# Down and out products with tokens as the stationary operand and rows turned back, a re-ordered first attention, and spread context scaling, in a two-block transformer kernel on one NeuronCore

## The chip, the core and the metric

The kernel runs on one core of one Trainium2 chip. The metric is the device time of one execution in microseconds (us), lower is better. TensorE multiplies matrices; the profile calls its matmuls PE and its loads of the stationary operand PEld. VectorE is DVE, ScalarE is ACT, GpSimd is POOL, and SyncE (SP) issues most of the DMA loads.

## What is computed

256 tokens of width 1024, all in float32, pass through two blocks. The first has two layers. What matters here of them:

```python
def swiglu_ffn(x, w_in, w_out):
    gate, up = jnp.split(x @ w_in, 2, axis=-1)
    return (jax.nn.silu(gate) * up) @ w_out
...
for layer in range(DEPTH):                       # DEPTH = 2
    normed = rms_norm(h, mix_norm_pre[layer])
    mixed = retention_mixer(...) if layer == 0 else nsa_mixer(...)
    h = h + rms_norm(mixed, mix_norm_post[layer])
    normed = rms_norm(h, ffn_norm_pre[layer])
    h = h + rms_norm(swiglu_ffn(normed, ...), ffn_norm_post[layer])
```

`retention_mixer` and `nsa_mixer` (16 heads: a compressed, a selected and a window branch, each with its softmax) end in an out projection. So there are four places where a product of width 1024 is normed over its features per token, gained, and added to `h`: after each mixer and after each feed-forward part. The second block (adaLN modulation from `c_2`, a gated MLP over chunks, window attention with a second context `ctx_2`, merge, and 16 experts by expert choice with 2048 hidden columns) follows. The experts' weights are some 400 MB and are read once.

## The kernel before, in words

**Layout.** `h` and everything that enters a product lie transposed: features on the 128 partitions, in 8 chunks, by 256 tokens (T). PSUM is `ps`, 8 banks of 512 float32 columns.

**Products in three parts.** A dense weight arrives in units of 1 MB (`ring`, 6 slots). ACT rounds a unit to fp32r (`split_hi`, L646), DVE takes what is left (`split_lo`, L654), and the same is done for tokens (L679, L684). TensorE then multiplies hi by hi, hi by lo and lo by hi. There are two buffers for split units, taken in turn (`SPLIT_NO[U] % 2`). `col_products` (L782) makes 256 new features from all 1024, in 48 matmuls of 256 columns. The first two units after a joint run together chunk by chunk (`pair_products`, L804), since their tokens come one chunk at a time.

**Down and out products.** `row_T` (L850) adds 256 input features of a unit to all 1024 outputs: the weight block of 128 x 128 is stationary and the 256 tokens stream, 8 output chunks x 2 x 3 = 48 matmuls, added up in four PSUM banks over all units. It is used by the retention's out product (8 units, `U_RO`), both feed-forward parts (11 units each, `PAIRS`), the first attention's out product (4 units, `NO_UNITS`), and by the last products of the second block (12 units at `U_PA`, `U_PB`, `U_WO`). `wide_tok` (L835) is the other form that the kernel has: a token block of 128 x 128 is stationary and 512 weight columns stream, 24 matmuls for a unit.

**The joints.** After each of the four sums comes a joint. ACT squares the four banks (L1655, L1660), DVE adds the squares (L2063), TensorE sums them over partitions by a matmul with `ones` (`norm`, L758), ACT takes the root (L1544), and DVE forms `h * root` and then the product's gained value plus that (L2106, L2109): the kernel keeps `h` multiplied by the post-norm's root and takes it out again later (`root_inverse`, L2045, and `over_root`, L2052), with one extra matmul per next norm for the epsilon (L749). ACT gains and rounds the new `h` (`tokens_hi`, L1558), DVE takes the rest (`gained_lo`, L2088), and `pair_products` starts. The second unit after a joint is split in quarters (L662, L673) by hand-placed calls.

**The first attention.** Each engine's order is written out by hand. For each of 16 heads: `n_scores` (TensorE, two heads per call, L1071, L1073), `n_max` (DVE adds the bias and takes the maximum, L2400, L2404), `n_exp` (ACT, L1782), `n_factors` (DVE, L2412, L2414), a scaling on POOL (L2831), `n_turn` (six transposes on TensorE, L1130 to L1132), `n_pout` (ACT, L1790), and, per pair, `n_values` (TensorE, L1147 to L1153) and `o_out` (DVE, L2418). `n_s` has four buffers. Between them stand units of the adaLN product (`ada`, L896), the splits of the four out units, and the first two `out_unit`s.

**The context.** `ctx_2` is loaded to `ctxn`, summed (L1218), and scaled in six POOL operations of 128 x 1024 (L2845) while the second feed-forward part runs. Its keys and values (L1234, L1240) are made at the fourth joint.

**The end.** Loads of expert weights (4 MB each) are queued on SP behind the dense units and wait for their memory to come free; from about 1,070 us the kernel computes experts as their weights arrive.

Of the kernel before, what the change touches and what calls it, by code (L numbers as in the profile page):

```python
# [13 lines left out]
P = 128  # L14
# [98 lines left out]
for _name, _n in [("ident", 128), ("perm", 128), ("tri", 128), ("slot", 32), ("fold", 18), ("ret_cos", T), ("ret_sin", T),  # L113
# [25 lines left out]
SUM_BANK = {N_PRE0: 4, N_POST0: 0, N_PREF0: 4, N_POSTF0: 0, N_PRE1: 4, N_POST1: 4, N_PREF1: 0, N_POSTF1: 4,  # L139
            N_IN2: 4}  # L140

ADDED = {N_PRE0: (0,), N_POST0: (0, 3), N_PREF0: (0,), N_POSTF0: (0, 3), N_PRE1: (0,), N_POST1: (0, 3),
         N_PREF1: (0,), N_POSTF1: (0, 3), N_IN2: (0, 3)}
# [3 lines left out]
AFTER_POST = {N_PREF0: 0, N_PRE1: 1, N_PREF1: 2, N_IN2: 3}  # L147
# [11 lines left out]
def program(nc, a, out):  # L159

    ctx = ExitStack()
    with ctx:
# [77 lines left out]
        eps_r2, rs_post = xn[:, 0, :], xn[:, 1, :]  # L240
# [112 lines left out]
        sq_half = sem("sq_of_next_to_last_chunk_ready")  # L353
        eps_ready = sem("eps_times_square_of_root_ready")
        h_true = sem("h_over_root_set")
# [360 lines left out]
        def gate_bank(f, j):  # L716
            return (0, 4)[f] + 2 * (j % 2)
# [17 lines left out]
        def _(pe):  # L735
# [9 lines left out]
            def norm(n):  # L745

                if n in AFTER_POST:
                    pe.wait_ge(eps_ready, AFTER_POST[n] + 1)
                    pe.matmul(ps[:, SUM_BANK[n], 0:T], ones[:], eps_r2, start=True, stop=False)  # L749
                for q in ADDED[n]:  # L750
                    if q == 0:
                        pe.wait_ge(sq_added, 2 * n + 2)
                    elif n not in POST_NO:
                        pe.wait_ge(sq_ready, 4 * n + q + 1)
                    for c in (2 * q, 2 * q + 1):
                        if q and n in POST_NO:
                            pe.wait_ge(*((sq_ready, 4 * n + 4) if c == 7 else (sq_half, POST_NO[n] + 1)))
                        mm = pe.matmul(ps[:, SUM_BANK[n], 0:T], ones[:], sq[:, c, :], start=c == 0 and n not in AFTER_POST,  # L758
                                       stop=c == 2 * ADDED[n][-1] + 1)
                mm.then_inc(ss_ready, 1)  # L760
# [95 lines left out]

            def row_pair(U0, u, n, x0, banks, free=None):
# [5 lines left out]
            def bias_table(half):  # L863
                if half == 0:
                    pe.wait_ge(btab_in, BTAB_IN)
                    pe.matmul(ps[0:HEADS, 3, 0:384], rel[0:33, 0:HEADS], bucket_rows, start=True,
                              stop=True).then_inc(brow_mm, 1)
                for i in range(N_CMP // 3):
                    j = half * (N_CMP // 3) + i
                    mm = pe.matmul(ps[:, 2, i * 3 * HEADS:(i + 1) * 3 * HEADS], bucket_cmp[:, j * P:(j + 1) * P], rel[:],  # L870
# [2132 lines left out]
```

## Time and profile before

| | |
|---|---|
| median of 3 runs | 1973.45 us (1972.36 to 1973.92) |
| the profiled execution | 1973.38 us, of which the span of its instructions is 1971.6 us |
| TensorE matmuls / weight loads | busy 1602.9 us / 1131.9 us, 11459 each |
| DVE, ACT, POOL | busy 769.2, 556.3, 112.2 us |
| HBM | 595.52 MB read, 304 GB/s over the span |

The times in the rows below are microseconds from the start of the span. A float32 matmul of this kernel shows as two rows (x2), an fp32r matmul as one. `L` numbers are lines of the kernel before.

### The profile page before, as it was taken

How to read it: one execution, taken by the hardware profiler on the slowest of the kernel's cores; microseconds unless marked ns; L12 is line 12 of the kernel's file. 1: busy time of each engine (PE TensorE's matmuls, PEld its weight loads, DVE VectorE, ACT ScalarE, POOL GpSimd, SP SyncE). 2: the span in 40 equal slices, each digit the busy share in tenths (PEclk: the TensorE clock that was granted, in tenths of full speed). 3: DMA queues.
4: the chain of work that ended last, by engine and by line, in shares of the span. 5: the costliest groups of instructions: out<-in, count | busy, mean ns of one | idle time of the engine just before them, and what ended most of it. 6: DMA issues, size and time to landing. Idle time of an engine off the chain costs nothing.

```text
span 1971.6 us, 26369 instructions
## 1 busy us (share of the span) xinstructions
PE 1602.9 (81%) x11459; PEld 1131.9 (57%) x11459; DVE 769.2 (39%) x1117; ACT 556.3 (28%) x881; POOL 112.2 (6%) x98
## 2 busy tenths in 40 slices
PE   7999999999899999999999756666555665565656
PEld 7899999998689999897897211111111111111112
DVE  6766776676658557768664100000000000000000
ACT  4454544354754435546562000000000000000001
POOL 1001000000403000003300000000000000000000
PEclk9999999999999999999999977777778778778878
DMA  9854597658265554452379999999999999999997
GB/s 353 307 176 159 142 318 256 216 169 277 69 255 211 192 178 164 140 181 86 100 299 379 419 433 428 433 430 432 430 430 431 432 431 431 430 432 432 429 434 313
DMA packets 100522, 604.32 MB, mean 307 GB/s; under 512 B 5340, under 2 KB 60821, under 8 KB 75336
## 3 DMA queue, kind: packets, MB, share of 16 engines
q1 hardware_dynamic: 91456, 587.22, 74.5%
q10 hardware_dynamic: 7832, 11.26, 1.9%
q0 software_dynamic: 1136, 4.40, 1.6%
q8 instruction: 77, 1.26, 0.3%
q14 instruction: 21, 0.17, 0.0%
HBM read 595.52 MB, written 4.20 MB: 304 GB/s over the span
## 4 chain that ended last, share of the span: by engine, by line
PE 55%; DMA 39%; DVE 4%; ACT 1%; issue 1%; POOL 0%; DVEq 0%; ACTq 0%
DMA _expert_slots_and_tokens<-in_experts 38%; PE ps L782 20%; PE ps L850 12%; PE ps L1478 4%; PE ps L835 3%; PE ps L1512 2%; PE ps L804 2%; PE ps L1296 2%; DVE split_operands L654 2%; PE ps L1058 1%; PE ps L1437 1%; PE ps L1320 1%; PE ps L1330 1%; PE ps L758 1%; PE ps L743 1%
## 5 line engine op out<-in xcount | busy, mean ns | idle before, releaser
L782 PE MATMUL ps<-split_operands 128*128 128x256 f32 x3360 | 412.2, 284 | 2.2 <-issue 1.2
L654 DVE TENSOR_TENSOR split_operands<-dense_ring_and_tables,split_operands 128x1024 fp32r<-128x1024 f32 x282 | 344.8, 1264 | 166.9 <-ACT split_operands L646 166.7
L782 PEld LDWEIGHTS ps<-split_operands 128*128 128x128 f32 x3360 | 406.4, 192 | 5.0 <-issue 2.9
L646 ACT ACTIVATE split_operands<-dense_ring_and_tables 128x1024 fp32r<-128x1024 f32 x282 | 282.6, 1050 | 299.3 <-PE ps L782 153.2
L2787 DVE TENSOR_TENSOR arena<-arena,ps 128x512 f32<-128x512 f32 x16 | 11.0, 688 | 562.9 <-PE ps L1478 562.9
L2008 ACT ACTIVATE arena<-ps 128x512 f32<-128x512 f32 x16 | 9.6, 597 | 571.6 <-PE ps L1478 571.6
L850 PE MATMUL ps<-split_operands 128*128 128x256 f32 x1248 | 152.3, 284 | 1.8 <-DVE split_operands L684 1.7
L850 PEld LDWEIGHTS ps<-split_operands 128*128 128x128 f32 x1248 | 150.4, 192 | 4.1 <-DVE split_operands L684 2.9
L850 PE MATMUL ps<-hidden_split,split_operands 128*128 128x256 f32 x960 | 118.6, 283 | 0.8 <-DVE split_operands L654 0.8
L850 PEld LDWEIGHTS ps<-hidden_split,split_operands 128*128 128x128 f32 x960 | 116.6, 192 | 1.0 <-DVE split_operands L654 1.0
L2794 DVE TENSOR_TENSOR tabs<-ps,tabs 128x512 f32<-128x512 f32 x16 | 11.1, 692 | 264.7 <-PE ps L1512 264.7
L1478 PE MATMUL ps<-_expert_slots_and_tokens,arena 128*32 128x512 f32 x400 | 69.9, 862 | 53.9 <-DMA _expert_slots_and_tokens<-in_experts 53.9
L1478 PE MATMUL ps<-dense_ring_and_tables,arena 128*32 128x512 f32 x416 | 69.3, 826 | 50.6 <-DMA dense_ring_and_tables<-in_experts 50.6
L1512 PE MATMUL ps<-dense_ring_and_tables,arena 128*32 128x512 f32 x384 | 63.7, 824 | 47.9 <-DMA dense_ring_and_tables<-in_experts 47.9
L1512 PE MATMUL ps<-_expert_slots_and_tokens,arena 128*32 128x512 f32 x432 | 68.0, 788 | 38.3 <-DMA _expert_slots_and_tokens<-in_experts 37.5
L1478 PE MATMUL ps<-_expert_slots_and_tokens 128*32 128x512 f32 x384 | 67.5, 867 | 36.9 <-DMA _expert_slots_and_tokens<-in_experts 36.9
L1478 PE MATMUL ps<-dense_ring_and_tables,_expert_slots_and_tokens 128*32 128x512 f32 x416 | 62.5, 753 | 36.0 <-DMA dense_ring_and_tables<-in_experts 35.9
L2012 ACT ACTIVATE tabs<-ps 128x256 f32<-128x256 f32 x16 | 6.2, 385 | 300.5 <-PE ps L1490 300.5
L1478 PEld LDWEIGHTS ps<-_expert_slots_and_tokens,arena 128*32 128x32 f32 x400 | 15.7, 150 | 108.1 <-DMA _expert_slots_and_tokens<-in_experts 65.7
L1478 PEld LDWEIGHTS ps<-dense_ring_and_tables,arena 128*32 128x32 f32 x416 | 16.0, 144 | 103.0 <-DMA dense_ring_and_tables<-in_experts 61.0
L1512 PEld LDWEIGHTS ps<-dense_ring_and_tables,arena 128*32 128x32 f32 x384 | 16.1, 144 | 90.5 <-issue 52.3
L1478 PEld LDWEIGHTS ps<-_expert_slots_and_tokens 128*32 128x32 f32 x384 | 18.1, 150 | 85.8 <-issue 85.8
(371 smaller groups left out, 1834.1 us busy)
## 6 DMA issues: line engine op xcount, KB each, us to landing
dense_ring_and_tables<-in_experts SPq DMA_DIRECT2D x36, 4096.0 KB, 43.1
_expert_slots_and_tokens<-in_experts SPq DMA_DIRECT2D x35, 4096.0 KB, 43.1
arena<-in_experts SPq DMA_DIRECT2D x17, 4096.0 KB, 43.1
dense_ring_and_tables<-in_ffn_units SPq DMA_DIRECT2D x66, 1024.0 KB, 4.9
dense_ring_and_tables<-in_ret_w_in SPq DMA_DIRECT2D x23, 1024.0 KB, 9.2
dense_ring_and_tables<-in_w_in SPq DMA_DIRECT2D x22, 1024.0 KB, 5.1
dense_ring_and_tables<-in_w_ada SPq DMA_DIRECT2D x12, 1024.0 KB, 7.3
arena<-in_experts SPq DMA_DIRECT2D x6, 2048.0 KB, 8.9
```

The lines of the kernel that those rows point to most:

```text
L646: act.activation(w_hi[:, n % 2, c], ring[U % RING][:, c], ACT.Copy).then_inc(hi_ready, 1)
L654: dve.tensor_tensor(w_lo[:, n % 2, c], ring[U % RING][:, c], w_hi[:, n % 2, c], ALU.subtract).then_inc(lo_ready, 1)
L743: pe.matmul(ps[:, bank, c0:c0 + P], ones[:], ones[:], start=True, stop=True)
L758: mm = pe.matmul(ps[:, SUM_BANK[n], 0:T], ones[:], sq[:, c, :], start=c == 0 and n not in AFTER_POST, stop=c == 2 * ADDED[n][-1] + 1)
L782: mm = pe.matmul(ps[:, bank, b * T:b * T + T], left, right, start=k == 0 and i == 0, stop=k == 7 and i == 2)
L804: mm = pe.matmul(ps[:, banks[v], b * T:b * T + T], left, right, start=k == 0 and i == 0 and b == 0, stop=k == 7 and i == 2, skip_group_che ...
L835: mm = pe.matmul(ps[:, banks[t], :], x[:, 4 * half + k, t * P:t * P + P], w[:, k, :], start=half == 0 and k == 0 and i == 0, stop=half == ...
L850: mm = pe.matmul(acc_chunk(banks, b), w[:, c, b * P:b * P + P], v[:, c, :], start=first and c == 0 and i == 0 and b % 2 == 0, stop=last an ...
L1058: mm = pe.matmul(ps[:, bank, b * T:b * T + T], w[:, k, b * P:b * P + P], x[:, k, :], start=k == 0 and i == 0, stop=k == 7 and i == 2)
L1296: mm = pe.matmul(ps[:, 7, b * T:b * T + T], w[:, k, b * P:b * P + P], x[:, k, :], start=k == 0 and i == 0, stop=k == 7 and i == 2)
L1478: mm = pe.matmul(ps[32 * j:32 * j + 32, bank, :], xe(k)[:, e * CAP:(e + 1) * CAP], sl[:, c, 512 * j:512 * j + 512], start=k == 0, stop=k == 7)
L1512: mm = pe.matmul(ps[32 * g:32 * g + 32, 6, :], e_hidT[:, m * P + 32 * (w - 8):m * P + 32 * (w - 8) + 32], sl[:, m, 512 * half:512 * half + ...
```

## The change

1. `row_tok` takes the place of `row_T` in 34 of the 46 units (`U_RO`, both feed-forward parts, `NO_UNITS`); the 12 units of the second block keep `row_T`. The sum then lies by tokens: bank `b` holds tokens `128 * (b // 2)` onward and features `512 * (b % 2)` onward.
2. At a joint the squares are summed along the row by the squaring instruction itself (`accum_out`), the root is one number per token, and its inverse is put on a diagonal matrix of 128 x 128. The four banks are copied to SBUF, and `turn_rows` multiplies them by the diagonal, 8 float32 matmuls of 128 x 128 for each half of the tokens: that turns the rows back to features by tokens and norms them. `norm` of the four sums, the epsilon matmul, `h * root`, `root_inverse` and `over_root` are gone. Some PSUM banks change place.
3. In the first attention the calls are put in another order on TensorE, ACT and DVE.
4. Each of the six context scalings on POOL waits for one more step of the feed-forward part.

```diff
+            def row_tok(U, x, banks, first, last, r=0, free=None):
+                n = SPLIT_NO[U]
+                hi, lo = [w.rearrange("p k n -> p (k n)").rearrange("p (c n) -> p c n", c=2) for w in parts_of(U)]
+                pe.wait_ge(lo_ready, r * 12 + (2 * n + 2))
+                for b in range(4):
+                    t, half = b // 2, b % 2
...
+                    for c in range(2):
+                        for i, (v, w) in enumerate(((x[0], hi), (x[0], lo), (x[1], hi))):
+                            mm = pe.matmul(ps[:, banks[b], :], v[:, c, t * P:t * P + P], w[:, c, 512 * half:512 * half + 512],
...
+            def turn_rows(n, t):
+                p = POST_NO[n]
+                pe.wait_ge(y_copied, 4 * p + 2 * t + 2)
+                pe.wait_ge(post_dve, 4 * p + 2 * t + 2)
+                for k in range(8):
+                    c = slice(k % 4 * P, k % 4 * P + P)
+                    mm = pe.matmul(turned_chunk(n, k)[:, t * P:t * P + P],
+                                   post_rows(2 * t + k // 4).rearrange("p c t -> p (c t)")[:, c], diag[:, t, :],
+                                   start=True, stop=True, skip_group_check=True)
...
-            norm(N_POSTF0)
+            turn_rows(N_POSTF0, 0)
+            warm(5, 4, 0)
+            turn_rows(N_POSTF0, 1)
             bias_table(1)
-            warm(10, 1, 0)
...
+                for b in range(4):
+                    t = b // 2
+                    if b < 3:
+                        act.wait_ge(acc_done, TOLD[n] + b + 1)
+                    else:
+                        taken(act, last)
+                    rows = ps[:, ACC[n][b], :].rearrange("p (c t) -> p c t", c=2)
+                    act.activation(xn[:, 2 + 2 * (b % 3):4 + 2 * (b % 3), :], rows, ACT.Square,
+                                   accum_out=pst[:, b:b + 1]).then_inc(sq_ready, 1)
+                    if b % 2:
+                        act.wait_ge(post_dve, 4 * POST_NO[n] + 2 * t + 1)
+                        act.wait_ge(sq_ready, 4 * n + b + 1)
+                        act.activation(pst[:, 6 + t:7 + t], pst[:, b:b + 1], ACT.Sqrt, scale=1.0 / D,
+                                       bias=pst[:, 4 + t:5 + t]).then_inc(root_ready, 1)
+                act.activation(post_rows(3), rows, ACT.Copy).then_inc(y_copied, 1)
...
+                        if b == 2:
+                            dve.wait_ge(landed[(U + 1) % RING], 16 * ((U + 1) // RING + 1))
+                            taken(dve, SPLIT_UNITS[SPLIT_NO[U + 1] - 2])
+                            dve.tensor_copy(w_hi[:, SPLIT_NO[U + 1] % 2, 0:UNIT // 4], ring[(U + 1) % RING][:, 0:UNIT // 4])
+                    dve.wait_ge(root_ready, ROOT_NO[n] + t + 1)
+                    finished(dve.reciprocal(pst[:, 8 + t:9 + t], pst[:, 6 + t:7 + t]))
+                    dve.tensor_scalar(diag[:, t, :], ident, pst[:, 8 + t:9 + t], None, ALU.mult).then_inc(post_dve, 1)
...
+                    pool.wait_ge(f_hidden, PAIRS + 4 + 3 * q + i)
```

**TensorE at the first joint** (retention's out product, then the first feed-forward part). Before:

```order
L850 MATMUL ps<-split_operands 128x256 x384
L758 MATMUL ps<-late_expert_slots_and_tokens,ones 128x256 x4
L866 MATMUL ps<-arena 16x384
L870 MATMUL ps<-arena 128x48 x5
L804 MATMUL ps<-split_operands 128x256 x96
L749 MATMUL ps<-late_expert_slots_and_tokens,ones 128x256
```

Now:

```order
L875 MATMUL ps<-split_operands 128x512 x192
L890 MATMUL ps<-late_expert_slots_and_tokens 128x128 x8
L757 MATMUL ps<-ones 128x128 x5
L890 MATMUL ps<-late_expert_slots_and_tokens 128x128 x8
L911 MATMUL ps<-arena 16x384
L915 MATMUL ps<-arena 128x48 x5
```

384 matmuls of 256 columns became 192 of 512; the four sums by `ones` became 16 matmuls of 128 columns with 5 of filling (`warm`) between them. The other three joints change alike; only the first two have the filling.

**DVE in the first attention**, between the scores of heads 8 to 11 (L2400 and L2404 belong to `n_max`, L2412 and L2414 to `n_factors`, L654 is a split of an out unit, L2418 is `o_out`). Before:

```order
L2412 SCALAR_TENSOR_TENSOR softmax_stats<-softmax_stats,nsa_gates 128x4
L2414 RECIPROCAL softmax_stats<-softmax_stats 128x4
L654 TENSOR_TENSOR split_operands<-dense_ring_and_tables,split_operands 128x1024 x2
L2400 ISA late_expert_slots_and_tokens,softmax_stats<-ps,arena 128x256
L2400 ISA softmax_stats 128x1
```

Now, at the same factors (of head 8), the second split is not there; it stands after the factors of head 15:

```order
L2451 SCALAR_TENSOR_TENSOR softmax_stats<-softmax_stats,nsa_gates 128x4
L2453 RECIPROCAL softmax_stats<-softmax_stats 128x4
L2457 COPY arena<-ps 128x256
L658 TENSOR_TENSOR split_operands<-dense_ring_and_tables,split_operands 128x1024 x2
L688 TENSOR_TENSOR split_operands<-arena,split_operands 128x512 x2
```

On TensorE `out_unit(0)` now follows `n_turn(14)` (it followed `n_turn(13)`), the four `ada` units stand one at a time between turns, and `n_values(p)` comes one or two turns later than it did.

## Rows read from the trace of the kernel before

**Rows 1.** The page: the chain that ended last, shares by engine.

```profile
PE 55%; DMA 39%; DVE 4%; ACT 1%; issue 1%; POOL 0%; DVEq 0%; ACTq 0%
```

**Rows 2.** Windows: us, busy PE, PEld, DVE, ACT, POOL, granted clock, DMA share, GB/s.

```profile
300.00:350.00 50.00, 50.00 (x419) 50.00 (x418) 33.95 (x33) 20.13 (x23) 0.00 (x0) 1.00 0.66 237
505.00:550.00 45.00, 38.50 (x295) 24.52 (x294) 27.32 (x122) 34.00 (x109) 21.52 (x22) 1.00 0.32 124
1060.00:1070.00 10.00, 10.00 (x67) 7.67 (x66) 4.74 (x13) 0.00 (x0) 0.00 (x0) 1.00 0.83 351
1130.00:1180.00 50.00, 29.50 (x176) 7.77 (x180) 0.69 (x1) 0.60 (x1) 0.00 (x0) 0.80 1.00 430
```

**Rows 3.** The chain in order of time (start us, us, what), products of one unit.

```profile
60.02 43.56 PE ps L835 x192
...
354.25 5.76 PE ps L850 x48
```

**Rows 4.** The chain: first and second joint.

```profile
219.62 1.99 PE ps L758 x8
224.38 13.26 PE ps L804 x96
238.93 11.64 PE ps L782 x96
...
417.61 1.97 PE ps L758 x8
420.63 2.30 PE ps L743 x20
422.93 11.51 PE ps L804 x96
435.74 5.83 PE ps L782 x48
```

**Rows 5.** Timeline: the pair products of the first joint, with the idle time before.

```profile
224.38 13.26 PE L804 MATMUL ps<-split_operands 128*128 128x256 f32 x96 [0.80 <-DVE split_operands L2088]
```

**Rows 6.** The chain: third joint.

```profile
579.58 1.97 PE ps L758 x8
...
597.20 0.43 PE ps L749 x2
...
598.49 1.61 PE ps L782 x13
```

**Rows 7.** Timeline, ACT and DVE: a bank squared, an accumulator read, a reciprocal, new `h`.

```profile
416.21 0.60 ACT L1655 ACTIVATE _expert_slots_and_tokens<-ps 128x512 f32<-128x512 f32 x1 [0.84 <-PE ps L850]
...
889.47 0.18 ACT L1930 ACTIVATION_READ_ACCUMULATOR arena<-arena,softmax_stats 128x1 f32 x1
...
890.77 0.17 DVE L2622 RECIPROCAL softmax_stats<-softmax_stats 128x2 f32<-128x2 f32 x1
...
420.71 0.48 DVE L2109 SCALAR_TENSOR_TENSOR _expert_slots_and_tokens<-ps,cols,_expert_slots_and_tokens 128x256 f32<-128x256 f32 x1
```

**Rows 8.** The chain: down units before and after the six context scalings.

```profile
610.07 5.76 PE ps L850 x48
...
646.93 5.76 PE ps L850 x48
```

**Rows 9.** Timeline: DVE's splits without and with a POOL operation beside them.

```profile
617.02 2.36 DVE L654 TENSOR_TENSOR split_operands<-dense_ring_and_tables,split_operands 128x1024 fp32r<-128x1024 f32 x2 [3.40 <-ACT split_operands L646]
621.73 2.41 POOL L2845 TENSOR_TENSOR arena<-arena 128x1024 f32<-128x1024 f32 x1 [25.48 <-DVE arena L2514]
622.72 5.34 DVE L654 TENSOR_TENSOR split_operands<-dense_ring_and_tables,split_operands 128x1024 fp32r<-128x1024 f32 x2 [0.40 <-ACT split_operands L646]
```

**Rows 10.** The page's DMA issues (KB each, us to landing), and the chain's first expert load.

```profile
dense_ring_and_tables<-in_ffn_units SPq DMA_DIRECT2D x66, 1024.0 KB, 4.9
...
1096.80 23.62 DMA _expert_slots_and_tokens<-in_experts
```

More of the change, by code:

```diff
@@ L865, in bias_table @@
                     pe.wait_ge(btab_in, BTAB_IN)
[L866 removed]
+                    pe.matmul(ps[0:HEADS, 5, 0:384], rel[0:33, 0:HEADS], bucket_rows, start=True,
                               stop=True).then_inc(brow_mm, 1)
@@ L1214, in _ @@
             out_unit(3)
-            norm(N_POST1)
+            pe.wait_ge(ada_mod, 3)
+            turn_rows(N_POST1, 0)
             pe.wait_ge(ctx_act, 3)
-            for c in range(8):
-                mm = pe.matmul(ps[:, 6, 0:T], ones[:], ctx_sq[:, c, :], start=c == 0, stop=c == 7)
+            for c in range(3):
+                pe.matmul(ps[:, 0, 0:T], ones[:], ctx_sq[:, c, :], start=c == 0, stop=False)
+            turn_rows(N_POST1, 1)
+            for c in range(3, 8):
+                mm = pe.matmul(ps[:, 0, 0:T], ones[:], ctx_sq[:, c, :], start=False, stop=c == 7)
             mm.then_inc(ctx_mm, 1)
             pe.wait_ge(wr_set, 2)
-            pe.matmul(ps[:, 7, 0:EXPERTS], ones[:], wr_sum, start=True, stop=False, skip_group_check=True)
+            pe.matmul(ps[:, 1, 0:EXPERTS], ones[:], wr_sum, start=True, stop=False, skip_group_check=True)
             by_half = gs2.rearrange("p (i m c) -> p c i m", i=2, c=2)
@@ L1650, in post @@
                 split_hi(act, U)
-                if n in JOINTS:
-                    act.wait_ge(landed[(U + 1) % RING], 16 * ((U + 1) // RING + 1))
-                for q in range(3):
-                    act.wait_ge(acc_done, TOLD[n] + q + 1)
-                    act.activation(sq[:, 2 * q:2 * q + 2, :],
-                                   ps[:, ACC[n][q], :].rearrange("p (c t) -> p c t", c=2),
-                                   ACT.Square).then_inc(sq_ready, 1)
-                taken(act, last)
@@ L2039, in inverse @@
             def inverse(n):
[L2040 removed]
+                dve.wait_ge(root_ready, ROOT_NO[n] + 1)
                 dve.reciprocal(rs[:], rs[:]).then_inc(rs_ready, 1)
                 dve.wait_ge(rs_ready, RS_NO[n] + 1)
[L2044 to L2054 removed]
             def add_squares(n):
@@ new lines, in post @@
+                quarter_lo_split(dve, n, 0)
+                for k in range(9):
+                    if k < 8:
+                        dve.wait_ge(y_turned, 4 * p + k // 2 + 1)
+                        dve.scalar_tensor_tensor(out=h[:, k, :], in0=turned_chunk(n, k), scalar=col(name, k),
+                                                 in1=h[:, k, :], op0=ALU.mult, op1=ALU.add).then_inc(h_ready, 1)
+                    if k == 0:
+                        quarter_lo_split(dve, n, 1)
+                        if next_name:
+                            gained_lo(x0, next_name, 0)
+                    elif next_name and k >= 2:
+                        gained_lo(x0, next_name, k - 1)
+                        if k in (5, 6):
+                            quarter_lo_split(dve, n, k - 3)
@@ L2280, in ffn @@
                 hidden_and_split(1)
-                if f == 0:
-                    told = root_inverse()
-                    over_root(told, 0)
-                    over_root(told, 1)
                 if between:
@@ L2293, in ffn @@
                         hidden_and_split(3, i)
-                if f:
-                    told = root_inverse()
-                    over_root(told, 0)
-                    over_root(told, 1)
                 gate(10)
@@ L2326, in _ @@
             kv_out(3)
-            told = root_inverse()
-            over_root(told, 0)
-            over_root(told, 1)
             dve.memset(kc, 0.0).then_inc(c_kvev, 1)
```

286 lines of the change are left out of this document (136 added, 150 removed).

## The prediction

> **What bounds the kernel now.** I read the chain of waits first: 55% of the span is TensorE and 39% is DMA, nearly all expert weights [rows 1]. The windows by stage say where. Up to about 1,060 us TensorE is busy all the time in most windows (50.00 of 50.00 us, at a granted clock of 1.00) while the DMA engines have a third of their time free; from 1,130 us it is the reverse, with a DMA share of 1.00 at 430 GB/s and TensorE at 29.5 of 50 us [rows 2]. Between them, in the window at 1,060 us, the DMA share is still 0.83: loads of experts wait for memory that the first phase holds [rows 2]. So the end is the moment at which the first phase lets the expert loads go, plus a fixed amount of bytes, and each microsecond won in the first phase comes off the end; the chain passes from TensorE to an expert load at 1,096.80 us [rows 10]. Everything that changes lies before 800 us. The sum is made against the profiled execution, 1973.38 us, which stands 0.07 us from the median; I take it for the median.
>
> **The products: -10.9 us.** A unit of `row_T` is 48 matmuls in 5.76 us, 120.0 ns for 256 columns. The kernel already has the form that `row_tok` takes, a token block stationary and 512 weight columns streaming: 192 in 43.56 us, 226.9 ns each [rows 3]. 24 of these are 5.44 us, so a unit gives 0.32 us, and 34 units give 10.9 us. Weight loads halve, but they hide beside the matmuls in both forms. The splits that feed a unit (DVE 2.36 us for two halves [rows 9]) fit in 5.44 us as in 5.76. The rows differ only in what 512 columns cost beside two times 256: 13 ns of 240.
>
> The Trainium skill, on its page "TensorE: Matmul & The Clock Gate" (Part 1, the question on 56 ns), gives a warm matmul N divided by 2.4 GHz plus about 2.5 ns. By that a unit would win 24 times 2.5 ns, 34 units 2.0 us, and the sum would end at 1968.1. The trace has about 13 ns over N / 2.4 GHz for both widths, so it disagrees, and I go by the rows.
>
> **The joints: +2.7 us.** E is the end of the last unit of a sum. Before, the gate units behind a joint start 19.3 us after E (219.62 to 238.93), 18.1 (417.61 to 435.74) and 18.9 (579.58 to 598.49) [rows 4, 6]. This is TensorE work one piece behind another; only the first joint holds waits, 0.80 us ahead of its pair products [rows 5] and 1.75 us in them (13.26 beside 11.51 us [rows 4]).
>
> Now, a turn of half the tokens is 8 float32 matmuls of 128 columns. The nearest row is the filling, 10 such matmuls in 2.30 us [rows 4], so 8 take 1.84 us and a joint pays 3.68. Five of the filling are 1.15 us. Gone at each joint are `norm` with 1.97 us [rows 4] and the epsilon matmul with 0.43 [rows 6]. So:
> - First: 3.68 + 1.15 - 1.97 - 0.43 - the 2.55 of waits, which the later start should cover: -0.1.
> - Second: 3.68 + 1.15 - 1.97 - 0.43 - the old filling of 2.30: +0.1.
> - Third and fourth: 3.68 - 1.97 - 0.43: +1.3 each. The context's work there only changes places.
>
> The question is whether the engines behind are in time, since the bare sum assumes it. For the second half of the tokens ACT squares the last bank and reads its sum (0.60 and 0.18 us [rows 7]), takes a root of one column (0.2, estimated from the small operations beside it), and copies the bank (0.6, as the square); DVE inverts (0.17 [rows 7]) and fills the diagonal (0.2, estimated alike). With the handovers that is E + 1.7 to 2.0. TensorE comes to it at E + 3.0, so the first turn and the filling cover it; without the filling, as in the third and fourth joint, three context matmuls of 256 columns (1.3 us at 0.43 each) do. Next late is the first token chunk: turned at E + 3.7, then 0.5 us each for `h` (0.48 [rows 7]), for rounding and for the rest, E + 5.5, while TensorE comes at E + 6.0 in the second joint and later in the others. There the margin is thin, and from chunk 4 on the quarter splits stand between the chunks. I put +0 on it and keep +2 us a joint for the range.
>
> **The first attention: -4 us.** In the window 505 to 550 us TensorE is idle for 6.5 us [rows 2]: work of 38.5 us stretched by waits. That is the most that an order can give. The least is a loss of 2.4: the moved split of 2.36 us [rows 9] then stands open in front of `out_unit(1)`, and nothing is won before it. What ends those waits is DVE in the middle of its heads with two splits of out units between them, slowed by POOL; one of the two now stands after the last head, under `out_unit(0)`. But ACT is busy 34.0 of 45 us there and serves the heads in strict turn, its load stays, the other split stays, and all of turn, scores and values pass three engines. I take -4, nearer the upper end since TensorE's own work is the larger load in that window. `n_turn(14)` before `out_unit(0)` only changes places. The moved split delays the load of a later ring slot, which here has the DMA share of 0.32 to itself.
>
> **The context scaling: -2.0 us.** From 610.07 to 646.93 us stand two rounds of gate, up and down units, 36.86 us, where 6 units of 5.76 make 34.56 [rows 8]: 2.3 lost. There six POOL operations follow each other, and a DVE split of 2.36 us takes 5.34 [rows 9]. Spread over six rounds, each meets one DVE split per round, and it waits up to some 2.4 us. TensorE needs the first half of it at the end of the running down unit and the second half 2.9 us later, so that fits, with 0 to 0.3 us lost each time. The gain is at most 2.3, at worst 0. The Trainium skill ("SBUF — State Buffer", Who interferes with whom) says that the second of a DVE and a GpSimd instruction which both need the shared pair blocks until the first is through, which the 5.34 us bear out. By it the delay per round can't pass one POOL operation.
>
> **At nothing**: `root_inverse`, `over_root`, `h * root` (DVE, under running units), the moved banks, the DVE ops at the end of the feed-forward parts: TensorE waits for none of them now.
>
> **Sum**: 1973.4 - 10.9 + 2.7 - 4.0 - 2.0 = 1959.2 us.
>
> **Rivals.**
> - *The joints show* (0.16): a chain of small operations across three engines takes 2 us longer than the cover at each joint, +8: 1967.2. For it: the chain per joint has more handovers than before, and margins of 0.5 us. Against: no operation in it is longer than the 0.60 us of a bank [rows 7], where the one taken out had `norm`, a root and `h * root` in a row.
> - *The attention keeps its waits* (0.13): the split that stays, and ACT, hold the pace: 1963.2.
> - *A wide matmul costs what two narrow ones do* (0.03): 240 ns for 512 columns, no gain in the units: 1970.1, the same as before within what can be measured. 43.56 us for 192 speak against it. The formula of the Trainium skill's page "TensorE: Matmul & The Clock Gate" comes near this case.
> - *Slower* (0.05): DVE now waits for the landing of the weight unit U + 1 ahead of the second diagonal. Before, only the pair products waited for it. A late unit would then stop the turn, `h`, all token chunks and the tables behind. A unit takes 4.9 us from issue to landing [rows 10]. If it is issued only as the last unit ends, each joint pays those 4.9, +19.6: 1978.8. It decides once the landing comes later than E + 1.3. Against it: the DMA share in the phase is about 0.66, and the ring has six slots.
>
> **How the numbers follow.** A difference under 0.2% (3.9 us) can't be told from none. The forecast holds 0.63. Faster: 0.63, 0.13, and three quarters of the 0.16: 0.88. Same: the rest of that and 0.03: 0.07. Slower 0.05. The low end has the attention at -6.5 and the joints at +1.2: 1955.2, and 0.7 below for what I set to nothing. The high end is the joint rival, 1967.5; beyond it lie 0.04 + 0.03 + 0.05.
>
> **What would show it.** Right: the new product line with 226 to 228 ns per matmul; the turn line about 1.84 us per eight; TensorE idle below 0.3 us at the joints; less than 3 us idle in the attention; two rounds at 620 us in 33.9 us; the last expert load 14 us earlier. Wrong: idle time of TensorE released by ACT or DVE in front of the turns or the pair products, an attention as long as now, or a first expert load that moves less than TensorE does.

## The result, and the profile after

The changed kernel takes 1962.56 us in the median of 6 runs (1961.31 to 1964.42), the kernel before beside it 1973.32 (1972.36 to 1976.63): 10.8 us less, ratio 0.9943 with the interval 0.9933 to 0.9953. In another set of runs on one chip it was 1962.65 beside 1973.38, ratio 0.9944 (0.9930 to 0.9957). The forecast was 1959.2.

The page of the profiled execution: the number of TensorE's matmuls fell from 11459 to 10731, its busy time by only 6.6 us, and the chain is shared out as in [rows 1].

```profile
span 1961.1 us, 24928 instructions
...
PE 1596.3 (81%) x10731; PEld 1094.5 (56%) x10731; DVE 746.9 (38%) x1097; ACT 559.5 (29%) x901; POOL 104.2 (5%) x98
...
PE 55%; DMA 39%; DVE 4%; ACT 1%; issue 0%; POOL 0%; DVEq 0%; ACTq 0%
```

The chain of the changed kernel in order of time (start us, us, what). L927 is the first unit, L875 the new `row_tok`, L890 `turn_rows`, L810 the pair products, L788 `col_products`, L841 `wide_tok`.

```profile
9.91 8.19 PE ps L927 x48
18.10 0.86 PE ps L764 x4
18.96 5.76 PE ps L788 x48
...
185.54 32.94 PE ps L875 x144
218.47 1.93 PE ps L890 x16
221.52 1.79 PE ps L890 x16
...
225.30 10.16 PE ps L810 x84
236.70 1.24 DVE split_operands L658
238.08 11.75 PE ps L788 x96
...
351.71 5.47 PE ps L875 x24
...
413.55 1.93 PE ps L890 x16
416.60 1.79 PE ps L890 x16
419.44 10.14 PE ps L810 x84
430.83 1.24 DVE split_operands L658
432.20 5.99 PE ps L788 x48
...
571.28 2.02 PE ps L890 x16
...
591.85 11.74 PE ps L788 x96
603.59 5.47 PE ps L875 x24
...
637.55 5.47 PE ps L875 x24
...
767.32 1.93 PE ps L890 x16
...
786.58 22.02 PE ps L841 x96
...
1086.01 24.27 DMA _expert_slots_and_tokens<-in_experts
```

How to read it: a unit is now 5.47 us where [rows 3] had 5.76. Eight turning matmuls take 1.93 and 1.79 us. Behind each pair product a DVE split stands in the chain that was not there in [rows 4]. The first expert load leaves 10.8 us earlier than in [rows 10] (1086.01 beside 1096.80), and the span is 10.5 us shorter, so the end has moved about as much as TensorE's phase.

Windows by stage, as in [rows 2]; the second is moved by the 3 us that the stage begins earlier. TensorE is still always busy in the feed-forward part, and in the attention 2.2 of 45 us are idle where 6.5 were.

```profile
300.00:350.00 50.00, 50.00 (x355) 47.12 (x354) 35.76 (x33) 21.21 (x24) 0.00 (x0) 1.00 0.67 248
502.00:547.00 45.00, 42.77 (x312) 27.02 (x312) 27.70 (x125) 35.65 (x111) 19.25 (x24) 1.00 0.33 120
```

Some of TensorE's waits up to 1,100 us (who waits, for whom: us in all, times, longest). The third and fourth lines are waits at the joints that the kernel before does not have: the third is one wait at each of the joints 1 to 3, the fourth stands ahead of the first turn of joint 3.

```profile
PE ps L1179 <- POOL arena L2867: 2.2, 3, 1.4
PE ps L875 <- DVE split_operands L688: 1.6, 2, 1.0
...
PE ps L788 <- DVE split_operands L658: 0.9, 3, 0.3
...
PE ps L890 <- DVE _expert_slots_and_tokens L2142: 0.2, 1, 0.2
```

**A common clock for the profiles.** The first unit of the kernel took 7.30 us in the profile before and 8.19 after, at the same 48 matmuls that the change doesn't touch. So I count from the start of the second unit (18.03 us before, 18.96 after; what differs ahead of it is told with the last run) and compare where each kernel then stands: at the end of each sum (E1 to E4) and where the joint behind it is over (the next whole unit starts).

| us from the second unit | E1 | joint 1 over | E2 | joint 2 over | E3 | joint 3 over | E4 | joint 4 over |
|---|---|---|---|---|---|---|---|---|
| before | 201.6 | 220.9 | 399.6 | 417.7 | 561.6 | 580.5 | 761.4 | 779.3 |
| after | 199.5 | 219.1 | 394.6 | 413.2 | 552.1 | 572.9 | 748.4 | 767.6 |
| difference | -2.1 | -1.8 | -5.0 | -4.5 | -9.4 | -7.6 | -13.0 | -11.7 |

The joints give back 0.3, 0.5, 1.9 and 1.3 us, 4.0 in all. The stretches between give 2.1, 3.2, 5.0 and 5.4. Behind joint 4 the difference stays at 11.7, to the first expert load (1078.8 before, 1067.1 after). A second profile of the changed kernel stands within 0.1 us of this row everywhere.

### The profile page after: what moved, and what is told of

Its sections match the earlier page's. It is cut to its first block, busy times and chain, and to the rows that moved or that the text cites. A ratio compares the mean times of both kernels' runs of the same rounds, so it can differ in the third digit from the quotient of the medians.

```text
span 1961.1 us, 24928 instructions
## 1 busy us (share of the span) xinstructions
PE 1596.3 (81%) x10731; PEld 1094.5 (56%) x10731; DVE 746.9 (38%) x1097; ACT 559.5 (29%) x901; POOL 104.2 (5%) x98
## 4 chain that ended last, share of the span: by engine, by line
PE 55%; DMA 39%; DVE 4%; ACT 1%; issue 0%; POOL 0%; DVEq 0%; ACTq 0%
DMA _expert_slots_and_tokens<-in_experts 39%; PE ps L788 20%; PE ps L875 9%; PE ps L1532 4%; PE ps L841 3%; PE ps L856 3%; PE ps L1350 2%; PE ps L1566 2%; PE ps L810 2%; DVE split_operands L658 1%; PE ps L1107 1%; PE ps L890 1%; PE ps L1491 1%; PE ps L1374 1%; PE ps L1384 1%; PE ps L757 1%
## 5 line engine op out<-in xcount | busy, mean ns | idle before, releaser
L788 PE MATMUL ps<-split_operands 128*128 128x256 f32 x3360 | 411.8, 284 | 2.1 <-issue 1.2
L788 PEld LDWEIGHTS ps<-split_operands 128*128 128x128 f32 x3360 | 407.4, 192 | 6.5 <-issue 4.0
L875 PE MATMUL ps<-split_operands,hidden_split 128*128 128x512 f32 x480 | 112.6, 390 | 0.0
L1532 PE MATMUL ps<-_expert_slots_and_tokens,arena 128*32 128x512 f32 x400 | 69.9, 862 | 50.6 <-DMA _expert_slots_and_tokens<-in_experts 50.6
L1566 PE MATMUL ps<-_expert_slots_and_tokens,arena 128*32 128x512 f32 x432 | 64.0, 747 | 43.2 <-DMA _expert_slots_and_tokens<-in_experts 42.5
L875 PEld LDWEIGHTS ps<-split_operands,hidden_split 128*128 128x128 f32 x480 | 88.8, 188 | 17.6
L1532 PE MATMUL ps<-dense_ring_and_tables,_expert_slots_and_tokens 128*32 128x512 f32 x416 | 67.6, 807 | 35.3 <-DMA dense_ring_and_tables<-in_experts 35.3
L1532 PE MATMUL ps<-_expert_slots_and_tokens 128*32 128x512 f32 x384 | 62.9, 814 | 37.9 <-DMA _expert_slots_and_tokens<-in_experts 37.9
L875 PE MATMUL ps<-split_operands 128*128 128x512 f32 x336 | 78.3, 391 | 1.6 <-DVE split_operands L688 1.6
L1532 PEld LDWEIGHTS ps<-dense_ring_and_tables,arena 128*32 128x32 f32 x416 | 16.1, 146 | 104.7 <-DMA dense_ring_and_tables<-in_experts 62.3
L875 PEld LDWEIGHTS ps<-split_operands 128*128 128x128 f32 x336 | 62.5, 188 | 16.5 <-DVE split_operands L688 2.4
L856 PE MATMUL ps<-split_operands 128*128 128x256 f32 x576 | 69.9, 283 | 0.6 <-DVE split_operands L688 0.5
L856 PEld LDWEIGHTS ps<-split_operands 128*128 128x128 f32 x576 | 69.3, 192 | 1.4 <-DVE split_operands L688 1.0
```

Of the source, the lines that this page charges most:

```text
L788: mm = pe.matmul(ps[:, bank, b * T:b * T + T], left, right, start=k == 0 and i == 0, stop=k == 7 and i == 2)
L856: mm = pe.matmul(acc_chunk(banks, b), w[:, c, b * P:b * P + P], v[:, c, :], start=first and c == 0 and i == 0 and b % 2 == 0, stop=last an ...
L875: mm = pe.matmul(ps[:, banks[b], :], v[:, c, t * P:t * P + P], w[:, c, 512 * half:512 * half + 512], start=first and c == 0 and i == 0, st ...
L1532: mm = pe.matmul(ps[32 * j:32 * j + 32, bank, :], xe(k)[:, e * CAP:(e + 1) * CAP], sl[:, c, 512 * j:512 * j + 512], start=k == 0, stop=k == 7)
L1566: mm = pe.matmul(ps[32 * g:32 * g + 32, 6, :], e_hidT[:, m * P + 32 * (w - 8):m * P + 32 * (w - 8) + 32], sl[:, m, 512 * half:512 * half + ...
```

## The experiments

Their profiles are counted in the same way.

**The scaling alone.** One line in the kernel before:

```diff
+                    pool.wait_ge(f_hidden, PAIRS + 4 + 3 * q + i)
```

> The kernel before with one added line: each of GpSimd's six operations of the context scaling waits for a pair of the second feed-forward. My theory (term of -2.0 in the prediction; the two traces give 36.86 us before and 33.96 after for the stretch of three pairs, of which 0.6 is the products' own): the time falls by 2.0 to 2.4 us, and the three-pair stretch beside the scaling goes from 36.9 to about 34.6. Rival (the stretch only moves its wait to the later pairs): the time falls by less than 0.7 us.

Measured: 1972.37 us beside 1975.14, ratio 0.9988 (0.9979 to 0.9997), a median 2.8 us lower where 2.0 to 2.4 were expected; the interval is far wider than that difference. Its chain, from down unit to down unit over the stretch of [rows 8], and the splits beside a POOL operation that the timeline shows:

```profile
609.80 5.76 PE ps L850 x48
...
644.36 5.76 PE ps L850 x48
```

```profile
662.45 1.90 POOL L2846 TENSOR_TENSOR arena<-arena,mod_gain 128x1024 f32<-128x1024 f32 x1 [14.80 <-DVE arena L2248]
...
662.77 3.78 DVE L654 TENSOR_TENSOR split_operands<-dense_ring_and_tables,split_operands 128x1024 fp32r<-128x1024 f32 x2 [0.41 <-ACT split_operands L646]
```

The stretch is 34.56 us, 6 units of 5.76 with nothing lost, 2.3 less than before. That alone would not rule out the rival, since the POOL operations now start at 645 us, behind this stretch. But TensorE shows no wait from 612 to 720 us, in which five of the six POOL operations fall, and from the end of joint 3 to E4 it takes 178.6 us instead of 180.9: the 2.3 are won and not moved. A split beside a POOL operation takes 3.78 us in the line shown (4.38 at most) where 2.36 is its own. The 1.4 us of delay lie under the 1.90 of the POOL operation beside it, as the bound allows that the prediction took from the Trainium skill ("SBUF — State Buffer", Who interferes with whom).

**The order alone.** The three call lists of the first attention (TensorE, ACT, DVE) from the changed kernel in the kernel before, for example:

```diff
-            split_lo(dve, NO_UNITS[1])
             n_max(11)
             n_factors(9)
...
             o_out(o_n, 5, 0)
+            split_lo(dve, NO_UNITS[1])
             o_lo(1)
```

> The kernel before with the order of the calls in the first attention alone, on TensorE, ScalarE and VectorE. My theory (term of -4.0, all of it TensorE's idle time there; the two traces put about 3.9 on it): the time falls by 3.5 to 4.3 us, TensorE's idle time between 505 and 550 us falls from 6.5 to about 2.2 us. Rival (the new order gains only together with the shorter out products, since these end the stretch): the time falls by 2 us or less.

Measured: 1970.3 us beside 1975.14, ratio 0.9978 (0.9969 to 0.9987), a median 4.8 us lower, 0.5 more than the upper end of what was expected. The trace gives less. E3 stands at 557.9 where the kernel before has 561.6, with no difference at E2: 3.7 us. All of TensorE's waits between 500 and 550 us, 6.5 us before, are now one line:

```profile
PE ps L1130 <- POOL arena L2831: 2.5, 3, 1.4
```

**The products alone.** `row_T` of the kernel before with the body of `row_tok`:

```diff
-                for b in range(8):
+                for b in range(4):
+                    t, half = b // 2, b % 2
...
-                        for i, (w, v) in enumerate(((hi, x[0]), (hi, x[1]), (lo, x[0]))):
+                        for i, (v, w) in enumerate(((x[0], hi), (x[0], lo), (x[1], hi))):
```

> The kernel before with the body of its 34 units of down and out products replaced by the new one: 24 matmuls over 512 weight columns in place of 48 over 256 token columns; the sums then stand by tokens where the rest reads them by features, so what follows computes other values in the same number of instructions. Theory by the trace of after (227.7 ns for one of 512 columns): 0.29 us less per unit, 9.9 us less in all. By my prediction's row (226.9 ns): 0.32 per unit, 10.9 less. Rival (TensorE's shorter units are waited out, since VectorE and ScalarE can't split faster): under 5 us less, with waits for the splits ahead of the units.

Measured: 1962.0 us beside 1975.14, ratio 0.9941 (0.9927 to 0.9954), a median 13.1 us lower. One thing in the expectation was not so: the edit sits in the function, so it also changed the 12 units of the second block, 46 and not 34. By 0.29 us each, 46 give 13.3. The trace shows the 34 alone where nothing disturbs them: -2.1 at E1 for 8 units, 3.2 more from there to E2 for 11. The rival falls as the main effect, since the gain is far over its 5 us. In part it is there: where a unit already had to wait for the split of its tokens, the wait grows. Ahead of the retention's third unit it is 1.01 us where it was 0.66, and in the second block, after 1,000 us, two waits of 0.37 and 0.70 us stand where one of 0.46 stood.

**All but the joints.** The three edits together in the kernel before, with the joints as they were.

> The kernel before with the wide products, the attention's new order and the spread scaling together, and the four joints as before (the values behind a joint are others, as in the run with the wide products alone). If the parts add up, it is 9.9 + 3.9 + 2.3 = 16.1 us faster than the kernel before, so some 5 us faster than the changed kernel (whose gain is 10.8): the joints' price measured by itself. By the prediction's term the joints cost 2.7, and this kernel would be 13.5 us faster than before. Rival (parts overlap, the spread scaling and the order gain nothing beside the shorter products): 11 us faster or less.

Measured: 1955.71 us, a median 19.4 us lower, ratio 0.9908 (0.9893 to 0.9924). The parts add up: 13.1 by the medians of the products alone and 2.3 + 3.7 by the traces of the other two are 19.1. By medians throughout they are 20.7, which the widths of the intervals allow as well. The 12 units of the second block, which the expectation left out, are in here too, by 3.0 us between joint 4 and the first expert load in its trace. Without them it is some 16 us, and the changed kernel has 10.8 in its own comparison: the joints cost about 5 us, and not the 2.7 of the prediction. The trace says the same. This kernel and the changed one are level at E1; after the four joints the changed one is 1.7, 2.2, 3.8 and 5.2 us behind.

**Joint 1 and the clock.** Why 5.2 here and 4.0 against the profile before? The rows of the 1.5 us are the granted clock (windows 224 to 228 us: us, busy PE, PEld, DVE, ACT, POOL, granted clock, DMA share, GB/s), first of the kernel before, then of the one with the scaling alone, which is the same program up to there:

```profile
224.00:228.00 4.00, 3.62 (x17) 3.62 (x18) 4.00 (x12) 3.04 (x6) 0.00 (x0) 0.57 0.00 0
```

```profile
224.00:228.00 4.00, 3.21 (x27) 3.08 (x27) 4.00 (x11) 2.89 (x7) 0.00 (x0) 1.00 0.00 0
```

The pair products took 13.26 us in the one ([rows 5]) and 11.77 in the other. So of the 1.75 us that the prediction called a wait inside them, 1.5 were matmuls at the lower of TensorE's two clocks (1.2 GHz) behind 0.80 us of idling: they start every 0.21 us there and every 0.12 us elsewhere. The other 0.26 are a matter of how the chain is read. Its piece begins where the matmul before ended; matmuls that follow without a wait overlap by some 0.2 us, and behind a wait that overlap is missing. Of the five profiles that have the old joint 1 and that idle time, three show this drop. I put filling in:

```diff
             bias_table(0)
+            warm(10, 1, 0)
```

> The kernel before with ten filling matmuls (1.1 us) ahead of the pair products of joint 1, as it has them at joint 2. Three of four profiles with the old joint 1 and the old place of its arrival show the granted clock at 0.57 to 0.87 for 1.5 us of it, and its pair products at 13.3 us instead of 11.8. Theory (the clock falls there because TensorE idles 0.8 us behind the post norm): no drop, 11.5 to 11.8 us. Rival (the drops come at random, as one at 460 us does in two of ten profiles): 13.3 us in this profile too.

Measured: a single execution, 1976.48 us. The drop at joint 1 is gone (granted clock 1.00, pair products 11.51 us), but the joint is over at 220.7 instead of 220.9: the filling takes 2.30 us, where the expectation had 1.1, and costs what it saves. This execution had another drop, at 514 us, and its first unit took 8.62 us where the profile before has 7.30; these two make up most of the 3 us by which it is slower. In none of the eight profiles where TensorE doesn't idle ahead of the pair products of joint 1 did the clock fall there. That supports idling as the cause at this place without proving it, as drops came at other places too, some of them with no idle time ahead.

**Unit 0 first.** In the changed kernel:

```diff
-                for k in range(6):
+                for k in range(4):
                     pe.wait_ge(xlo_ready, x0 + k + 1)
                     chunk(0, k)
                     chunk(1, k)
-                for k in range(6, 8):
+                for k in range(4, 8):
```

> The changed kernel with another order in the first products behind joints 1 to 3: both units for input chunks 0 to 3, then unit 0 for chunks 4 to 7 and only then unit 1 for them. Unit 0 is so given up after 72 of the 96 matmuls instead of 84, 12 x 120 ns = 1.4 us sooner, while its input chunks come no later than now. Theory (TensorE waits 0.3 us at each of these joints for the split of the unit that takes unit 0's place): those three waits are gone, the three stretches from the pair's start to the next unit's are 12.4 us and not 12.7, 0.9 us in all. Rival (the wait is for something else, or the input chunks now arrive too late): the stretches stay at 12.7 or grow.

Measured: a single execution, 1960.58 us. TensorE's waits from 200 to 650 us are the two lines below, so the three for the split are gone, and joint 4 is over at 766.0 instead of 767.6. That is 1.6 us, more than the 0.9: the piece behind the joint, L788 x96, is now 11.51 us in the chain instead of 11.75. It holds no second wait: in both traces its matmuls start every 0.12 us. It is the overlap with the matmuls before, which a wait costs besides its own length. Each joint gains 0.3 ahead of that piece and some 0.2 in it.

```profile
PE ps L1179 <- POOL arena L2867: 2.2, 3, 1.4
PE ps L890 <- DVE _expert_slots_and_tokens L2142: 0.2, 1, 0.2
```

**The epsilon matmul back.**

```diff
+                for q in ADDED[n]:
+                    pe.wait_ge(*((sq_ready, 4 * n + q + 1) if q else (sq_added, 2 * RS_NO[n] + 2)))
+                pe.matmul(ps[:, SUM_BANK[n], 0:T], ones[:], sq[:, 0, :], start=True, stop=True)
                 norm(n)
```

> The changed kernel with one more matmul of 256 float32 columns (0.43 us) ahead of the norm's sum behind the pair products of joints 1 to 3, where the kernel before had its eps matmul. Theory (0.3 us of it lie beside the wait for the next unit's split): the joints grow by 0.1 to 0.15 each, and the wait of 0.3 is gone. Rival (the eps matmul was worth its full 0.43): they grow by 0.4 each, with the wait still there.

Measured: a single execution, 1962.5 us. Joints 1 and 2 are over at 219.2 and 413.3 (219.1 and 413.2 without), and joint 3 takes 20.7 us from its first turn on, 20.6 without. The wait for the split is gone. So 0.43 us of TensorE's work cost 0.1 at the joint, and at the end of the next sum nothing: E2 stands at 394.6 with and without it. This execution also had a clock drop at 508 us, which cost it 0.3 us ahead of joint 3.

**No filling.**

```diff
-            warm(5, 5, 0)
...
-            warm(5, 4, 0)
```

> The changed kernel without the ten filling matmuls between the two turns at joints 1 and 2. Theory (bank copy 3 and diagonal 1 are ready 1.7 us after the products' end, when the first turn ends at 1.8, so the 1.1 us of filling stand on the path): each of the two joints is 1.0 to 1.1 us shorter, 19.6 and 18.65 us become about 18.5 and 17.6, and no wait stands ahead of the second turn that is longer than 0.1. Rival (the filling hides the wait for the copy and the diagonal, or the input chunks set the pace of the pair products behind it): less than 0.4 us each.

Measured: a single execution, 1962.02 us. Joint 1 falls from 19.6 to 18.6, joint 2 from 18.65 to 17.7, and the two turns stand back to back. The chain of this kernel at joint 1:

```profile
218.40 3.87 PE ps L890 x32
...
224.25 10.15 PE ps L810 x84
```

But of the 1.9 us only 0.3 are left at E3. Between joint 2 and there the granted clock was 0.78 and 0.79 in the two windows from 456 to 464 us, 1.6 us of the same kind as above:

```profile
456.00:460.00 4.00, 4.00 (x30) 3.34 (x30) 2.90 (x4) 3.98 (x9) 0.00 (x0) 0.78 0.86 215
```

The run with the wide products alone, which has the filling, had a drop at that place too.

**The context's squares on VectorE.**

```diff
+            dve.wait_ge(ctx_act, 3)
+            for c in (4, 2):
+                finished(dve.tensor_tensor(ctx_sq[:, 0:c, :], ctx_sq[:, 0:c, :], ctx_sq[:, c:2 * c, :], ALU.add))
+            dve.tensor_tensor(ctx_sq[:, 0, :], ctx_sq[:, 0, :], ctx_sq[:, 1, :], ALU.add).then_inc(ctx_added, 1)
...
-            for c in range(3, 8):
-                mm = pe.matmul(ps[:, 0, 0:T], ones[:], ctx_sq[:, c, :], start=False, stop=c == 7)
+            pe.wait_ge(ctx_added, 1)
+            mm = pe.matmul(ps[:, 0, 0:T], ones[:], ctx_sq[:, 0, :], start=True, stop=True)
```

> The changed kernel with the context's eight squares added up by VectorE (three additions, about 1.9 us, while it is idle ahead of the modulation) so that TensorE sums them with one matmul at joint 3 in place of eight. Theory (TensorE's own work fills joint 3 from the end of the products to the pair products, the input chunks are there 2.4 us before): joint 3 falls from 20.8 to about 17.8 us, 7 matmuls x 0.43. Rival (once they are gone TensorE waits for the first input chunk or for the additions): joint 3 falls by 1.5 us or less, and the additions delay the modulation and the bank copies.

Measured: a single execution, 1959.26 us. Joint 4 is over at 764.7 (767.6), 3.0 earlier. From its first turn on joint 3 takes 17.6 us (552.4 to 569.9) instead of 20.6, all of the 3.0. The timeline of DVE shows the additions in time (the modulation's first operation, L2188, starts at 565.61 where it started at 565.63):

```profile
562.04 1.95 DVE L2518 TENSOR_TENSOR arena<-arena 128x1024 f32<-128x1024 f32 x2 [1.69 <-ACT arena L1907]
564.03 0.42 DVE L2519 TENSOR_TENSOR arena<-arena 128x256 f32<-128x256 f32 x1
565.61 0.26 DVE L2188 TENSOR_TENSOR mod<-ps,cols 128x16 f32<-128x16 f32 x2 [1.16 <-PE ps L959]
```

**All together**, with the modulation's small operations behind the bank copies of joint 3 (called between the quarter split and the first `h`). And the changed kernel itself again on the same chip.

> The changed kernel with the three edits of the runs before (unit 0 first, no filling at joints 1 and 2, the context's squares added by VectorE) and a fourth, by which the small operations of the modulation stand behind the bank copies of joint 3 and not ahead of them (0.2 us of TensorE's wait there). If they add up as their profiles give them: 1.6 + 1.9 + 3.0 + 0.2 = 6.7 us less than the changed kernel, about 1956, or 17.5 us (0.9%) less than the kernel before. Rival (without the filling TensorE's clock falls more often behind the joints, 1.6 us each time as in the run without it): 5 us less than the changed kernel, or little more than the additions' 3.0.

> The changed kernel itself once more, to be compared with the combined one on one chip, and for a second profile of it. The ratio to the kernel before should be within 0.9933 to 0.9953 again. If the first unit's 8.2 us (7.3 before) and the missing clock drop at joint 1 belong to the change, both are the same here; if they differ from one execution to another, the first unit lies anywhere from 7.2 to 8.7 us, as in the other six profiles.

Measured: 1956.16 us (1955.26 to 1956.35, 4 runs) beside 1973.38, ratio 0.9909 (0.9894 to 0.9924); the changed kernel 1962.65 (1962.14 to 1963.26). So 6.5 us less where 6.7 were expected, and 17.2 less than the kernel before. Joint 4 is over at 761.3 (767.6), and TensorE no longer waits ahead of the first turn of joint 3. No drop of the clock shows in the profile up to 1,090 us, and its runs lie within 1.1 us, so the rival falls for this kernel. The first unit of the changed kernel took 7.25 us this time and 8.19 before: it lies between 7.25 and 8.65 in the 13 profiles, whatever the kernel. The 0.9 us are no part of the change. They are TensorE's clock too. Windows of the two profiles of the changed kernel (us, busy PE and its matmuls for the first unit alone, granted clock, DMA share, GB/s), first that with 8.19 us, then that with 7.25:

```profile
12.00:14.00 2.00, 2.00 (x11) 1.00 1.22 394
```

```profile
12.00:14.00 2.00, 2.00 (x15) 1.00 1.17 376
```

The matmuls start every 0.21 us at first, as in the drop at joint 1, and every 0.12 us from 14.9 us on in the one and from 12.8 us in the other. So some 22 and some 12 of the 48 are slow ones, and ten times 0.09 us is the difference. The granted clock reads 1.00 in these windows all the same, since the trace has no clock record from before the rise.

## Why the prediction was right, and where it was off

The direction, the parts and the order of their sizes came as worked out; the sum was 3.4 us too low: 1.2 in the products, 1.3 in the joints, and 0.9 that only the medians have. The misses of 0.2 in the attention and in the scaling have opposite signs, and that they cancel is luck. Two numbers of the text don't come out of its own terms: -0.1, +0.1 and two times +1.3 are +2.6 for the joints and not +2.7, and the high end of 1967.5 is given as the joint rival, which comes to 1967.2.

- **The products, -10.9: 9.7 measured.** 34 units take 5.47 us each and not 5.44. The row of 192 matmuls gave 226.9 ns; the new ones take 227.7, so a unit gives 0.29, and 34 would give 9.9. The retention's eight gave a little less, 2.1 and not 2.35. There the term left out a wait: the third unit's tokens, split by DVE, don't come as much earlier as TensorE does, and TensorE's idle time ahead of that unit grew from 0.66 to 1.01 us. Timeline of TensorE, before and after:

```profile
184.81 34.81 PE L850 MATMUL ps<-split_operands 128*128 128x256 f32 x288 [0.66 <-DVE split_operands L684]
```

```profile
185.54 32.94 PE L875 MATMUL ps<-split_operands 128*128 128x512 f32 x144 [1.01 <-DVE split_operands L688]
```

The Trainium skill ("TensorE: Matmul & The Clock Gate", Part 1, the question on 56 ns) has some 2.5 ns over N / 2.4 GHz. The measured 227.7 ns are 14 over, and by that figure the gain would have been 2.0 us. The trace does not agree with it.
- **The joints, +2.7: 4.0 against the profile before.** This is the term that failed. The turns themselves were right (1.93 and 1.79 us for eight, 1.84 forecast) and joint 4 was right (+1.3 for +1.3). Three steps were not.
  - "the epsilon matmul with 0.43" was counted as gone at joints 1 to 3. It is gone, but it stood beside a wait. The split of the next unit can begin only when unit 0 of the pair is given up, and ends 0.3 us after TensorE has come to the next unit. So its removal was worth 0.1, as the run with a filler shows, and that 0.1 is lost again in the unit behind, which starts without overlap. The timeline of joint 2 shows the order: ACT's split starts when L810 gives unit 0 up, DVE follows, TensorE waits for it.

```profile
429.66 2.00 ACT L650 ACTIVATE split_operands<-dense_ring_and_tables 128x1024 fp32r<-128x1024 f32 x2 [2.84 <-PE ps L810]
...
430.83 2.36 DVE L658 TENSOR_TENSOR split_operands<-dense_ring_and_tables,split_operands 128x1024 fp32r<-128x1024 f32 x2 [2.21 <-ACT split_operands L650]
...
432.20 2.03 PE L788 MATMUL ps<-split_operands 128*128 128x256 f32 x15 [0.34 <-DVE split_operands L658]
```

  - "the 2.55 of waits" at joint 1: 1.5 of them were the clock drop and not a wait. Against the profile before they did go (+0.3 for -0.1), by the luck that it had the drop. Against executions without the drop the joint costs 1.8, the four joints 5.2 to 5.5.
  - The third joint has 0.2 us more, the first turn's wait for DVE (the run of all together, which moves those operations, has no such wait). The small operations of the modulation and a split of 2.36 us stand ahead of its bank copies. I had looked only at the second half of the tokens.
- **The margins** that I put at +0 held. At joint 2 the second turn could have begun at E + 1.7 (bank copy until 415.14, diagonal until 415.25, E at 413.55), as estimated, and came at E + 3.05. The first chunk was ready 0.8 us before TensorE came. The rival in which the joints show falls for its mechanism: nothing waits for the chain of small operations behind the last bank. What I missed is that the margin made the filling pure cost, 1.0 us a joint.

```profile
414.57 0.57 ACT L1716 ACTIVATE _expert_slots_and_tokens<-ps 128x512 f32<-128x512 f32 x1
...
414.96 0.29 DVE L2153 TENSOR_SCALAR _expert_slots_and_tokens<-tabs,_expert_slots_and_tokens 128x128 f32<-128x128 f32 x1
```

- **The attention, -4.0:** 3.8 by the stations, 3.7 alone. TensorE idles 2.2 of 45 us, for POOL's scaling now. The rival that keeps the waits falls.
- **The scaling, -2.0:** 2.2 in the changed kernel beyond the shorter products (33.96 us for two rounds, the text had 33.9), 2.3 alone. The 0 to 0.3 us a round that I allowed did not occur.
- **A wide matmul at the price of two** falls: 227.7 ns and not 240. **DVE's wait for the landing** falls: no wait of TensorE at a joint comes from a late unit, and at joint 2 the diagonal was ready at E + 1.7.
- **The end:** an expert load as much earlier as TensorE held: 11.7 us on the common clock.
- **The signs.** Right were the turns, the attention (2.2 us idle) and the two rounds (33.96 us), and the product line within its 226 to 228 ns. Not met were the load 14 us earlier (10.8) and TensorE's idle time below 0.3 us at the joints (0.3 at joints 1 and 2, 0.5 at joint 3). One sign of being wrong was there in small: 0.2 us of idle time released by DVE in front of a turn.

The sum by rows is 9.7 + 3.8 + 2.2 - 4.0 = 11.7, the medians give 10.8. The clock at joint 1 goes the right way for the 0.9 between them: the profile before is one of those with the 1.5 us drop, and only three of five have it, which on average is 0.6 less. It is not shown more directly than that, and the other 0.3 stay open.

## What to carry to other kernels

- Before counting a removed instruction as won, ask which event the next one on its engine needs. If a buffer is given up late in front of it, the removed work was cover. Then move the giving-up, not the work: 12 matmuls put behind it were worth 1.6 us here.
- A stretch that takes longer than its matmuls need not be a wait: read the granted clock of that window and the spacing of the matmuls (0.12 or 0.21 us here) before naming a releaser.
- A unit that gets shorter gains less where its operand's split was already waited for: count the waits ahead of it, not only its length.
- Filling that keeps TensorE busy costs nearly its full length (1.0 of 1.1 us) once what it waits for is ready. Work of TensorE that another engine does in its idle time (eight squares added before they are summed: 3.0 us) was the cheapest gain in this case.

## What the runs showed of the hardware that I had not expected

- The granted clock falls for a few microseconds in some executions of the same program. The places seen: 224 us (3 profiles), 456 to 464 us (2), 508 to 520 us (3). Seven of these eight cost 1.5 to 1.7 us; the one at 508 us in the run with the epsilon matmul cost only 0.3, since TensorE would have waited for POOL right behind it. In that run TensorE had not waited since 200 us, and at 456 us it was busy all the time too, so idling is not the only way to a drop. Elsewhere up to 1,090 us no profile shows one.
- The first unit after the start takes 7.25 to 8.65 us for the same 48 matmuls, which take 5.76 later. In the two profiles of the changed kernel the difference is the number of matmuls that still run at the slower spacing (some 22 for 8.19 us, some 12 for 7.25). One profile's start can so differ from the next by over 1 us with no cause in the code, about the size of what a joint costs.
